# Finer weight fetches for the last three experts, the last gated product in two halves, and the last LayerNorm's statistics on VectorE

## What is computed

```
h1 = layer_norm(ALPHA * h + mix)                      # 288 rows x 1024
logits = h1 @ w_router + b_router                     # 32 experts, top 4 of them, softmax -> gates
for e in range(32):
    gu   = h1 @ w1[e] + b1[e]                         # w1[e]: 1024 x 2048, fp32, 8 MB
    gate = minimum(gu[:, :1024], 7)
    up   = clip(gu[:, 1024:], -7, 7)
    act  = (up + 1) * (gate * sigmoid(1.702 * gate))
    out += gates[:, e] * (act @ w2[e] + b2[e])        # w2[e]: 1024 x 1024, fp32, 4 MB
y = layer_norm(ALPHA * h1 + out)
```

## Time and profile before

| what | us |
|---|---|
| median of three runs | 1128.57 |
| the profiled execution, its own time | 1127.28 |
| its span, first to last instruction | 1125.5 |
| PE busy in the span | 1054.6 (94%) |
| DVE / ACT busy | 395.4 (35%) / 234.3 (21%) |
| mean rate of the DMA queues | 375 GB/s |
| mean granted PE clock | 0.986 |

### The profile page before, as it was taken

How to read it: one execution, slowest core, us unless ns; L and a number is a source line. 1 busy time by engine, 2 the same in 40 slices (tenths; PEclk the granted TensorE clock), 3 DMA queues, 4 the chain that set the end, 5 groups by cost and what they waited for, 6 DMA issues and landing times.

```text
span 1125.5 us, 13844 instructions
## 1 busy us (share of the span) xinstructions
PE 1054.6 (94%) x5298; PEld 437.2 (39%) x5299; DVE 395.4 (35%) x689; ACT 234.3 (21%) x470; POOL 15.4 (1%) x26
## 2 busy tenths in 40 slices
PE   8989998999999998999999999999999999999995
PEld 7765454333333333333333333333333333333331
DVE  7682356333333332333333333322223322233234
ACT  3234210111222211111111111111111111111122
POOL 1003000000000000000000000000000000000000
PEclk9999898999999999999999999999999999999998
DMA  9750333999999999999999999999999999999981
GB/s 321 271 225 1 115 150 132 427 429 429 429 429 429 429 428 438 431 433 430 430 431 437 430 433 430 430 431 437 432 431 430 430 433 434 433 430 430 428 377 42
DMA packets 27692, 421.82 MB, mean 375 GB/s; under 512 B 5229, under 2 KB 5869, under 8 KB 11450
## 3 DMA queue, kind: packets, MB, share of 16 engines
q1 hardware_dynamic: 27482, 420.93, 88.3%
q10 hardware_dynamic: 192, 0.66, 0.2%
HBM read 420.11 MB, written 1.46 MB: 375 GB/s over the span
## 4 chain that ended last, share of the span: by engine, by line
PE 49%; DMA 41%; DVE 7%; issue 1%; ACT 1%; SPq 0%; DVEq 0%; ACTq 0%
DMA ring<-in_w_dram 41%; PE ps L855 27%; PE ps L877 7%; PE ps L586 4%; PE ps L703 3%; PE ps L897 1%; DVE area L1583 1%; PE ps L565 1%; DVE area L1574 1%; DVE area L1577 1%; DVE area L1570 1%; PE ps L847 1%; PE ps L836 1%; DVE area L1571 1%; PE ps L650 1%
## 5 line engine op out<-in xcount | busy, mean ns | idle before, releaser
L855 PE MATMUL ps<-ring,area 128*64 128x512 f32 x2048 | 453.7, 597 | 22.9 <-DMA ring<-in_w_dram 22.9
L855 PEld LDWEIGHTS ps<-ring,area 128*64 128x64 f32 x2048 | 149.7, 138 | 309.6 <-issue 257.3
L877 PE MATMUL ps<-ring,area 128*64 128x512 f32 x1024 | 233.6, 599 | 0.0
L1570 DVE TENSOR_SCALAR area<-ps 128x512 f32<-128x512 f32 x32 | 22.1, 691 | 384.4 <-PE ps L855 384.4
L1583 DVE TENSOR_TENSOR area<-area,ps 128x1024 f32<-128x1024 f32 (+1 forms) x96 | 116.5, 1214 | 52.0 <-PE ps L897 52.0
L877 PEld LDWEIGHTS ps<-ring,area 128*64 128x64 f32 x1024 | 70.1, 137 | 126.1 <-issue 123.7
L1198 ACT ACTIVATE area<-area 128x512 f32<-128x512 f32 x32 | 20.1, 630 | 443.0 <-DVE area L1570 443.0
L1562 DVE SCALAR_TENSOR_TENSOR y_sb<-ps,gcol,y_sb 64x512 fp32r<-64x512 f32 x62 | 46.5, 751 | 98.4 <-ACT y_sb L1163 98.0
L897 PE MATMUL ps<-y_sb,giveT 128*128 128x512 f32 x192 | 69.4, 443 | 11.9 <-DVE area L1583 11.9
L827 PE MATMUL ps<-area 128*64 128x512 bf16 x558 | 66.1, 382 | 0.0
L1163 ACT ACTIVATE y_sb<-ps,gcol 64x512 fp32r<-64x512 f32 x62 | 42.3, 683 | 92.4 <-PE ps L877 91.7
(11 more groups left out here) (229 smaller groups left out, 628.2 us busy)
## 6 DMA issues: line engine op xcount, KB each, us to landing
ring<-in_w_dram SPq DMA_DIRECT2D x66, 4096.0 KB, 20.0
ring<-in_w_dram SPq DMA_DIRECT2D x60, 2048.0 KB, 15.6
area<-in_w_o_dram SPq DMA_DIRECT2D x1, 4096.0 KB, 13.0
area<-in_w_in_dram SPq DMA_DIRECT2D x1, 2560.0 KB, 16.5
area<-in_w_in_dram SPq DMA_DIRECT2D x1, 2336.0 KB, 9.4
area<-in_w_in_dram SPq DMA_DIRECT2D x1, 2048.0 KB, 20.6
lnb<-in_ln_g_dram SPq DMA_DIRECT2D x3, 512.0 KB, 10.2
lnb<-in_ln_b_dram SPq DMA_DIRECT2D x3, 512.0 KB, 11.6
```

The lines of the kernel that those rows point to most:

```text
L855: last = mm(ps_gu[g * BLK:(g + 1) * BLK, c, :], x[:, spot(k), :], half_of(w, c, g), start=False, stop=(k == KT - 1))
L877: last = mm(ps_y[g * BLK:(g + 1) * BLK, :], hT[:, c, h, :], w2_t[:, h, c, g * 512:(g + 1) * 512], start=False, stop=(h == 1 and c == 3))
L1570: v.tensor_scalar(g_sb, ps_gu[:, 0, :], LIMIT, None, ALU.min).then_inc(gate, 1)
```

## The change

It does five things.

1. The 4 MB fetches end with expert 28 instead of expert 30. Experts 29, 30 and 31 are fetched in 2 MB pieces. (Expert 31 was before.)
2. In the last expert, the gated product is made in two halves of 256 columns. A half (`quads(w, q)`) is two of every four neighbouring columns, so that it holds the two contraction steps 2q and 2q+1 of each slot of w2. Each half has its own clips, products, sigmoid, transposes, copy and down products.
3. The matmuls of the last down product are in another order: half 0 with slot 4, the transposes of half 1, half 0 with slot 5, `combine` of tile 1, half 1 with slots 4 and 5. The two bias matmuls stand ahead, and no longer wait for the copy.
4. All statistics of the last LayerNorm are on VectorE, and ScalarE's queue of the tail holds only roots, scalings and stores. The dummy `Sqrt` stands after the second copy of the turned product.
5. `keep_warm`: four filler matmuls ahead of the routing's `gate_split` wait, at about 174 us, and two and three in the last expert (each counted twice by the profile).

The diff, cut to these:

```diff
+    PAST_WIDE = 29
@@ sync
-            with sp.Fori(FIRST_WIDE, NE - 1) as e:
+            with sp.Fori(FIRST_WIDE, PAST_WIDE) as e:
                 for s in range(0, NSLOT, 2):
                     load_pair(e, s)
-            for s in range(NSLOT):
-                load(NE - 1, s)
+            for e in range(PAST_WIDE, NE):
+                for s in range(NSLOT):
+                    load(e, s)
@@ tensor
+            def turn_half(q):
+                pe.wait_ge(half_h, q + 1)
+                for c in (2 * q, 2 * q + 1):
+                    last = tr(ps[:, 7, c * P:(c + 1) * P], h_sb[:, c:512:4], ident[:, :])
+                last.then_inc(half_turned, 1)
+
+            def down_half(q, h):
+                pe.wait_ge(half_hT, q + 1)
+                for c in (2 * q, 2 * q + 1):
+                    for g in range(2):
+                        last = mm(ps_y[g * BLK:(g + 1) * BLK, :], hT[:, c, h, :],
+                                  w2_t[:, h, c, g * 512:(g + 1) * 512],
+                                  start=False, stop=(q == 1 and h == 1 and c == 3))
+                return last
...
             turn_x(x_first_sb, 1, x_gathered)
+            keep_warm(4)
             pe.wait_ge(gate_split, 1)
...
                     combine(2, comb_done[2], dst=ps_sum[2])
+                    keep_warm(2, bank=4)
                     pe.wait_ge(last_give, 1)
-                    pe.wait_ge(h_ready, NE)
-                    turn_h(ps[:, 7, :]).then_inc(hT_done, 1)
-                    pe.wait_ge(gate_ready, NE)
-                    pe.wait_ge(up_ready, NE)
+                    turn_half(0)
+                    keep_warm(3, bank=4)
+                    for g in range(2):
+                        a = 2 * F + g * 512
+                        mm(ps_y[g * BLK:(g + 1) * BLK, :], sel[:, :], bias_parts[:, a:a + 512],
+                           start=True, stop=False)
+                    pe.wait_ge(w_in_slot[4], 16 * NE)
+                    down_half(0, 0)
+                    turn_half(1)
+                    pe.wait_ge(w_in_slot[5], 16 * NE)
+                    down_half(0, 1)
+                    pe.wait_ge(half_gate, 2)
+                    pe.wait_ge(half_up, 2)
                     combine(1, comb_done[1], dst=ps_sum[1])
-                    pe.wait_ge(hT_ready, NE)
-                    down_products(e, 0, True)
-                    down_products(e, 1, True)
+                    down_half(1, 0)
+                    down_half(1, 1).then_inc(slot_free[5], 1)
@@ scalar, last expert
+                    act.wait_ge(slot_free[0], NE)
                     copy(x_giveT, ps_g[:, 0:TOKP])
                     nc.scalar.activation(gate_cols[:, :], ps_g[:, TOKP:TOKP + 3], ACT.Copy,
                                          accum_out=gcol[:, :]).then_inc(last_give, 1)
-                    nc.scalar.activation(tail[:, 3:4], eps[:, :], ACT.Sqrt)
-                    act.wait_ge(hT_done, NE)
-                    copy(hT, ps[:, 7, :].rearrange("p (c h s) -> p c h s", c=4, h=2)).then_inc(hT_ready, 1)
+                    for q in range(2):
+                        act.wait_ge(half_gate, q + 1)
+                        nc.scalar.activation(quads(sig_sb, q), quads(g_sb, q), ACT.Sigmoid,
+                                             scale=SWIGLU_ALPHA).then_inc(half_sig, 1)
+                        act.wait_ge(half_turned, q + 1)
+                        copy(hT[:, 2 * q:2 * q + 2],
+                             ps[:, 7, 2 * q * P:2 * (q + 1) * P].rearrange("p (c h s) -> p c h s", c=2, h=2))\
+                            .then_inc(half_hT, 1)
+                    nc.scalar.activation(std[:, 0:1], eps[:, :], ACT.Sqrt)
@@ vector, last expert
+            def swiglu_half(q):
+                g_q, u_q = quads(g_sb, q), quads(u_sb, q)
+                dve.wait_ge(slot_free[3], NE)
+                v.tensor_scalar(g_q, quads(ps_gu[:, 0, :], q), LIMIT, None, ALU.min).then_inc(half_gate, 1)
+                v.tensor_scalar(u_q, quads(ps_gu[:, 1, :], q), LIMIT, -LIMIT, ALU.min, ALU.max).then_inc(half_up, 1)
+                dve.wait_ge(half_gate, q + 1)
+                dve.wait_ge(half_up, q + 1)
+                v.scalar_tensor_tensor(u_q, u_q, 1.0, g_q, ALU.add, ALU.mult).then_inc(half_prod, 1)
+                dve.wait_ge(half_prod, q + 1)
+                dve.wait_ge(half_sig, q + 1)
+                v.tensor_tensor(quads(h_sb, q), u_q, quads(sig_sb, q), ALU.mult).then_inc(half_h, 1)
@@ vector, the tail
+            statistics(0)
             centre(0)
+            statistics(1)
             centre(1)
-            dve.wait_ge(act_step, 4)
-            link(v.reciprocal(rstd[0:TS, 2:3], std[0:TS, 2:3]))
+            statistics(2)
+            dve.wait_ge(scaled, 2)
+            v.tensor_tensor(halves(out_acc[:, 1, :]), ps_sum[1], halves(lnb[:, 1, :]), ALU.add).then_inc(result[1], 1)
+            centre(2)
```

More of the change, by code:

```diff
@@ L316, in encoder_kernel @@
         centred = sem("centred")
+        half_gate = sem("half_gate")
+        half_sig = sem("half_sig")
+        half_up = sem("half_up")
+        half_prod = sem("half_prod")
+        half_h = sem("half_h")
+        half_turned = sem("half_turned")
+        half_hT = sem("half_hT")
         scaled = sem("scaled")
-        act_step = sem("act_step")
         x_pick_ready = sem("x_pick_ready")
@@ L373, in spot, with quads @@
             return k % 4 * 2 + k // 4
+        def quads(w, q):
+            return w.rearrange("p (m c) -> p m c", c=4)[:, :, 2 * q:2 * q + 2]
         def proj_bank(i):
@@ L532, in _ @@
             pool.wait_ge(ln_in[2], 32)
-            with pool.Fori(FIRST_WIDE, NE - 1) as e:
+            with pool.Fori(FIRST_WIDE, PAST_WIDE) as e:
                 for s in range(0, NSLOT, 2):
@@ L859, in up_products, with turn_h @@
                 return last
-            def turn_h(dst=ps_hT):
+            def turn_h():
                 for c in range(4):
-                    last = tr(dst[:, c * P:(c + 1) * P], h_sb[:, c:512:4], ident[:, :])
+                    last = tr(ps_hT[:, c * P:(c + 1) * P], h_sb[:, c:512:4], ident[:, :])
                 return last
@@ L1231, in _ @@
             expert(NE - 1, last=True)
-            total, minus_mean, square = (tail[0:TS, i:i + 1] for i in range(3))
-            act.wait_ge(sum_ps[2], 1)
-            nc.scalar.activation(out_acc[0:TS, 2, :].rearrange("p (g n) -> p g n", g=2), ps_sum[2][0:TS, :, :], ACT.Copy,
-                                 accum_out=total).then_inc(act_step, 1)
-            act.wait_ge(act_step, 1)
-            nc.scalar.activation(minus_mean, total, ACT.Copy, scale=-1.0 / D).then_inc(act_step, 1)
-            sqrt_of(2 * NT, (0,))
-            act.wait_ge(act_step, 2)
-            nc.scalar.activation(out_acc[0:TS, 2, :].rearrange("p (g n) -> p g n", g=2), ps_sum[2][0:TS, :, :], ACT.Square,
-                                 bias=minus_mean, accum_out=square).then_inc(act_step, 1)
-            act.wait_ge(act_step, 3)
-            nc.scalar.activation(std[0:TS, 2:3], square, ACT.Sqrt, scale=1.0 / D, bias=eps[0:TS, :]).then_inc(act_step, 1)
+            sqrt_of(2 * NT, (0,))
             act.wait_ge(norm_ready, NT + 1)
@@ L1604, in expert @@
                     one_hot(pick, place[:, :, col(e + 1)], first_slots).then_inc(pick_ready, 1)
-                swiglu(slot_free[3], gate_ready, sig_ready, up_ready, prod_ready, e + 1, h_ready)
                 if last:
+                    for q in range(2):
+                        swiglu_half(q)
                     for t in range(NT):
@@ L1626, in _, with halves, statistics @@
             dve.wait_ge(ln_in[2], 32)
-            def centre(t):
+            def halves(at):
+                return at.rearrange("p (g n) -> p g n", g=2)
+            def statistics(t):
+                n = tiles[t][1]
                 dve.wait_ge(sum_ps[t], 1)
                 for q in range(2):
-                    ins = v.bn_stats(stats[:, t, q, :], ps_sum[t][:, q, :])
+                    ins = v.bn_stats(stats[0:n, t, q, :], ps_sum[t][0:n, q, :])
                 link(ins)
-                link(v.bn_aggr(moments[:, t, :], stats[:, t, :, :]))
-                v.tensor_scalar(veps[:, t:t + 1], moments[:, t, 1:2], LN_EPS, None, ALU.add).then_inc(var_ready, 1)
-                v.scalar_tensor_tensor(out_acc[:, t, :].rearrange("p (g n) -> p g n", g=2), ps_sum[t],
-                                       moments[:, t, 0:1], lnb[:, 0, :].rearrange("p (g n) -> p g n", g=2),
-                                       ALU.subtract, ALU.mult).then_inc(centred, 1)
+                link(v.bn_aggr(moments[0:n, t, :], stats[0:n, t, :, :]))
+                v.tensor_scalar(veps[0:n, t:t + 1], moments[0:n, t, 1:2], LN_EPS, None, ALU.add).then_inc(var_ready, 1)
@@ L1639, in centre @@
+            def centre(t):
+                n = tiles[t][1]
+                v.scalar_tensor_tensor(halves(out_acc[0:n, t, :]), ps_sum[t][0:n], moments[0:n, t, 0:1],
```

(3 more changed lines are left out.)

16 lines of the change are left out of this document (7 added, 9 removed).

## The result

The changed kernel took 1121.44 us, median of four executions (1121.18 to 1122.56), against 1128.76 for before beside it: ratio 0.994, 95% interval 0.9927 to 0.9953. The median of all nine is 1121.92. Forecast was 1123.3 in 1120.9 to 1126.0, faster.

The account below looks back on a forecast made before the run. Weight fetches set the pace, then the last two experts run as a PE chain, then the tail. Product 3.1 plus tail 2.15 make 5.25 us: 1123.3 us against a median of 1128.57, range 1120.9 to 1126.0.

Parts of the forecast that it names:

- the new waits: In expert 31, PE would wait about 0.4 us for slot 3 and about 0.6 us for slot 5.
- the product's term: Expert 31's last down product would end 3.1 us earlier, 1.8 of it from the up products.
- Fetches: Experts 29 and 30 lose their waits, 2.4 us; expert 31 gives some back; its up products end 1.8 us earlier.
- The fixed cost of a DMA: Six extra fetches at 2.0 us each would add 12 us to the stream; not adopted; as a rival, chance 0.01.
- Halves: Expert 31's gated product: each half takes about 1.76 us on VectorE, half 0 ready at 1092.0, half 1 at 1093.7.
- Now no idle stretch is longer than that 0.6 us: Last down product: short PE gaps keep the clock full; if it falls, the old 1.6 us comes back.
- Tail: Last LayerNorm: last store issued 6.2 us after the last sum instead of 8.36, a gain of 2.15 us.
- Early fillers: Four pairs, 1.1 us, in a 1.59 us wait before expert 0: no effect, at most 1.1 us cost without cover.
- Rival 2: Early fillers keep the clock up in expert 0, so the weight stream starts earlier: 1120.4 us, chance 0.1.
- the fourth: Rival: short fetches of experts 29 to 31 lose rate; at 390 GB/s the time is 1130.8 us; chance 0.03.

Follow-up runs that it names:

- fetches only: The kernel before with 2 MB fetches for experts 29 and 30 as well, nothing else: 0.997 of before, median 1124.92 us.
- fetches and tail: The kernel before with the finer fetches and the new last LayerNorm, gated product whole, last product in old order, no new filler: median 1122.20 us.

## Why the prediction was right

It named the direction, the size (5.25 forecast, 6.0 from the first fetch to the end, 7.3 and 4.3 between the medians of two sets) and the new waits. The fetches and the tail came as forecast in mechanism; the product's term came out by a clock that its own reason doesn't account for. Step by step:

- **Fetches: right, in mechanism and size.** The waits in experts 29 and 30 went; the experts run 27.93 us apart. The rate was 427 GB/s for 428 assumed, slot 5 landed 0.6 us later (against the stream's start) for 0.4 assumed (the prediction's own 58.8 less 58.3 is 0.5), expert 31 waits 0.62 for 0.4. Up products end at 1090.7, forecast 1090.2, of which 0.2 is the later start. One reading needs care: 1.2 us is not a saving that each further expert with short fetches would bring. An expert's 12.6 MB take 29.1 us at 432 GB/s, which is the 29.14 of the earlier trace rows, and PE alone takes 27.93. So the stream goes on setting the pace, and short pieces only let PE follow it more closely, once, until it stands for slot 3 of expert 31. The prediction allowed for that when it gave back 0.4 there.
- **The fixed cost of a DMA: rightly left out.** The Trainium skill's 2.0 us per DMA ("DMA: Bandwidth & Descriptors", "Anatomy of one DMA — SWDGE (gpsimd) path") was fitted for single DMAs on GpSimd's path, and these fetches are issued by SyncE, so the section didn't speak of them. Here such a cost doesn't stand in the stream of queued fetches: with six more of them slot 5 landed 0.6 us later in all.
- **Halves: durations right, attribution wrong.** 256 strided columns take 0.42 to 0.43 us, half 0 is ready 1.76 us after the start, and slot 5 is what comes next late (0.51, forecast 0.6). The product ends 2.4 us earlier than before (2.6 against the stream's start), 3.1 forecast. But the step "Now no idle stretch is longer than that 0.6 us", given as the reason for a full clock, credits the clock's 1.6 us to halves and fillers. The runs show it full with the old gap of 1.88 us (fetches only), full without fillers, and fallen with the same gap (fetches and tail). The halves do remove that gap. In the nine profiled executions of kernels with halves the fall didn't occur, in four of the five with the gap it did; that the halves make it rarer is likely, but not shown. In the executions compared, 1.5 of the product's 2.6 us are the clock: that this part came as forecast is in part luck.
- **Tail: the mechanism right, the term too small.** 2.15 forecast, 3.3 measured alone. The last store was issued 5.6 us after the last sum, not 6.2. The terms listed in the prediction add up to 6.0, so 0.2 of that is rounding; the other 0.4 is that it added VectorE's operations at full length, while in the trace most start about 0.07 us before the one ahead has ended. Besides, the last store landed in 2.0 instead of 2.6 us, which the sum left as it was.
- **Early fillers: nothing**, as forecast. Rival 2 (the clock in expert 0 sets the stream's start) was right that the clock in expert 0 moves the start of the stream, and wrong that these four fillers reach it. Ten behind the transposed picks went with a full clock in one profiled execution and with a fallen one in the other.
- The errors partly met: in the changed kernel the tail gave 3.4 us, 1.2 more than its term, and the product 2.6, 0.5 less.
- Small slips in the rivals' sums change nothing: the fourth's 7.3 us on top give 1130.6, not 1130.8, and an end of the product at 1109.5, not 1109.7.

Why the parts don't add up: alone they give 3.3, 3.3 and 1.5, in sum 8.1, together 6.0. The clock's 1.5 us is in two of them and can be had once. The rest, 0.6, is the wait for slot 5: once the product starts earlier, the stream's last piece is late.

## What to carry to other kernels

Look for the event that starts the bounding stream and measure from it to the end: here it took a scatter of 2 us out of every comparison and showed differences of a few tenths. When a stream of fetches sets the pace, cut its last pieces small, then put all work that doesn't need the last piece ahead of it; splitting work finer without moving it past the late wait gave nothing. And of a gain that several parts can each bring, count it once.

## What the runs showed that was not expected

- The granted clock at a given place differs between executions of one program: 0.51 between 166.4 and 169.8 us in one execution of before, 1.00 there in another, with the same instructions. That made 1.4 of the 2.7 us by which expert 0 started later; most of the rest came with a lower clock between 71 and 83 us.
- The same gap of 1.88 or 1.89 us ahead of the same work was followed by a fall in four profiled executions and by none in a fifth.
- 32 partitions take what 128 do on VectorE in the centring (1.26 and 1.27 us for 1024 columns).
